# Turning the expert table's blocks elsewhere: 16 in the output projection, 8 in retrieval, and the sum of squares moved to GpSimd

## The chip, the cores and the metric

The kernel runs on one core of one Trainium2 chip. The metric is the device time of one execution in microseconds (us), the median over several runs. It is one program: a hand-written order of instructions for each engine (TensorE, VectorE, ScalarE, GpSimd, and SyncE, which issues most of the DMAs), tied together by semaphores.

## The reference, cut to what matters

The kernel computes one layer of a streaming encoder for 512 prompt and 32 sample frames (T = 544 columns), model width 2048. After attention and the recurrent branch, the part in question is

```python
h = x + mixed @ w_out                               # output projection
xn = rms_norm(h, norm2_g)                           # needs the sum of h*h over the 2048 channels
q = (xn @ w_q).reshape(n, 8, 2, 128)                # retrieval: 8 heads
s1, s2 = q[:, :, 0] @ k1.T, q[:, :, 1] @ k2.T
... top 16 of each, top 16 of their sums -> idx, gate
h = h + peer_ffn(...)                               # rows of peer_u and peer_v picked by idx
```

`peer_u` (16384 x 2048 floats) is used twice: block by block as a weight of dense products, and, for 160 of the frames, by gathering single rows. For the gathers it is needed in another layout than that of the blocks.

## The kernel before, in words

The activations stand transposed, 16 slices of 128 channels x 544 frames. A **unit** is one 128 x 2048 block of a weight (1 MB) times all of them: 16 slices, each in three products (high part by high, high by low, low by high) and, for 544 columns, in two pieces, so 96 matmuls. Each unit passes through `Stream` (L119): `load` (L145) brings the raw block into one of two buffers; `split_hi` (L150) on ScalarE rounds it to its high part `whi`; `split_lo` (L154) on GpSimd subtracts and gives `wlo`; then TensorE may start (L236). The load of unit c waits until unit c-2 is split, `split_hi` of unit c until TensorE has used unit c-2.

**Rows** (L178) is the other stream: 128 blocks of `peer_u` are loaded (L204), turned by VectorE in 32x32 squares (L210, `STREAM_TRANSPOSE`) and written to a buffer in DRAM, `u_d`, by four DMAs of 256 KB (L220), from where the experts gather rows. The 128 turns are spread over the stages: 64 in attention, 32 in the recurrent branch, 8 in `mix`, 24 in `out_projection`. All DMAs of both streams stand in SyncE's queue in the order in which the code writes them; a wait there holds back all behind it.

`out_projection` (L1436) has 16 units, in pairs. Unit 0's product is done at the end of `mix`, so its PE part begins with unit 1. For each unit n: VectorE adds the product to X (L1520) and then turns one block (even units) or two (odd units), over three buffers; ScalarE squares the slice (L1505) and splits the weight of unit n+2; TensorE adds the square of the slice before into a PSUM bank by a product with ones (L1477, `add_squares`), 18 times in all. SyncE begins with the four loads of X (L1451), three block loads and the weight of unit 2; then for each unit: the weight of unit n+2, and for each turn its four stores and the next block load. The weight of unit 2 is thus the eighth transfer, and that of unit 3 stands behind the stores of the first turn.

After it comes `norm` "n2", and then `retrieval` (L1525): for each of 8 heads, two units of `w_q` with 544 columns, ten small products with the keys, two dense units of `peer_u` with 384 columns (48 matmuls each); VectorE runs a long chain that finds the top 16 (L1707 to L1752); eight more dense units follow while VectorE makes the gates. After the eighth head ScalarE's exponential (L1681) stands behind six of these units.

Of the kernel before, what the change touches and what calls it, by code (L numbers as in the profile page):

```python
# [48 lines left out]

LEVELS = [2, 4, 8, 16, 32]  # L50

AT_ROWS, RW_ROWS, MX_ROWS, WO_ROWS = 64, 32, 8, 24
GBUF = 4


# [189 lines left out]
def build(nc, A, O):  # L245
    ctx = ExitStack()
    with ctx:
# [35 lines left out]
        with ExitStack() as back:  # L283
            sbk = lambda n, s, d=F32: back.enter_context(nc.sbuf_tensor(n, s, d))

            at_hh = nc.sbuf_base
            hh, hl = sbk("hh", [P, KB, T], F32R), sbk("hl", [P, KB, T], F32R)
            assert nc.sbuf_base == at_hh + 2 * KB * T * 4
            load_h = lambda a, b: h_d[a:b].rearrange("k p t -> p k t")
            rows = mix(nc, S, A, W.phase(base["mix"]), [A["w_out"][0], A["w_out"][1]], acc, psS, psR, hh, hl, gates_d, o_d, u_d, rows,  # L290
                       lambda pe: unit_product(pe, W.phase(base["out"]), 0, acc[0], hh, hl))
            with ExitStack() as ctx2:
                X = ctx2.enter_context(nc.sbuf_tensor("X2", [P, KB, T], F32))
                out_projection(nc, S, A, W.phase(base["out"]), [A["u"][0], A["u"][1]], acc, psS, hh, hl, X, u_d, rows)
                W2 = W.phase(base["n2"])

                def two_units(pe):
                    for c in range(2):
                        yield from dense_product(pe, W2, c, acc[c][:, 0, 0:TD], hh, hl)
                norm(nc, S, "n2", A, par, eps, psS, X, C_N2, hi=hh, lo=hl, keep=load_h, summed=True, W=W2, then=two_units,  # L300
                     following=[A["w_q"][0], A["w_q"][1]])
            IDX, GT = sbk("IDX", [P, P], U32), sbk("GT", [P, P])
            IDXB, GTB = sbk("IDXB", [P, DEC], U32), sbk("GTB", [P, DEC])
            with ExitStack() as picks:
                IT = picks.enter_context(nc.sbuf_tensor("IT", [P, 3, TD], F32))
                iota = picks.enter_context(nc.sbuf_tensor("iota", [P, P], F32))
                retrieval(nc, S, A, W.phase(base["retrieval"]), [A["u"][TAIL], A["u"][TAIL + 1]], acc, psS, psR, hh, hl, IT, iota, IDX, GT, IDXB, GTB, pre_d)
                gate_matrix(nc, S, A, W.phase(base["gates"]), [A["u"][PRE - 2], A["u"][PRE - 1]], acc, psS, psR, hh, hl, IT, iota, g_d, pre_d)
            H = sbk("H", [P, KB, T])
            experts(nc, S, A, W.phase(base["experts"]), accs, psS, psR, H, load_h, hh, hl, IDX, GT, IDXB, GTB, g_d, pre_d, u_d, at_hh)  # L310
            norm(nc, S, "nf", A, par, eps, psS, H, C_NF, out=O["yT"], summed=True)
# [1124 lines left out]
def out_projection(nc, S, A, W, ahead, acc, psS, mh, ml, X, u_d, before):  # L1436

    with ExitStack() as ctx:
        sb = lambda n, s, d=F32: ctx.enter_context(nc.sbuf_tensor(n, s, d))
        SQ, ones = sb("wo_SQ", [P, 2, T]), sb("wo_ones", [P, P])  # L1440
        UI, UO = sb("wo_UI", [P, 3, D]), sb("wo_UO", [P, 3, D])
        N = 2
        R = Rows(S, A, u_d, lambda b: UI[:, b, :], lambda b: UO[:, b, :], before, 1, 3, KB // N, 3, 3)
        halves = lambda t: t.rearrange("p (h t) -> p h t", h=2)
        flat = lambda k: X[:, bass.ds(k, 1), :].rearrange("p a t -> p (a t)")
        block = ctx.enter_context(nc.Block())

        @block.sync
        def _(sp):
            for q in range(4):  # L1450
                sp.dma_start(X[:, 4 * q:4 * q + 4, :], A["xT"][:, 4 * q:4 * q + 4, :]).then_inc(S[f"n1loaded{q}"], 16)  # L1451

            def block_pair(i, last):
                for u in range(N):
                    W.load(sp, ahead[u] if last else row(A["w_out"], N * i + u + 2), u + 2, N, i)
                    for c in range(1 + u):
                        R.store(sp, u + c, i)
                        if not last:
                            R.load(sp, u + c + 3, i)
            for c in range(3):  # L1460
                R.load(sp, c)
            with sp.Fori(0, KB // N - 1) as i:
                block_pair(i, False)
            block_pair(KB // N - 1, True)
            R.finish(sp)

        @block.gpsimd
        def _(pool):
            with pool.Fori(0, KB // N) as i:
                for u in range(N):  # L1470
                    W.split_lo(pool, u + 2, N, i)

        @block.tensor
        def _(pe):
            def add_squares(u, start=False):
                for half in range(2):
                    mm = pe.matmul(psS[:, half, 0:H2], ones[:, :], SQ[:, u, half * H2:(half + 1) * H2], start=start, stop=True,  # L1477
                                   skip_group_check=True)
                mm.then_inc(S["wo_summed"], 1)
            pe.wait_ge(S["wo_set"], 2)  # L1480
            add_squares(1, True)

            def block_pair(i, first=False):
                for u in range(N):
                    if not first or u:
                        pe.wait_ge(S["wo_sum"], N * i + u + 1)
                        for mm in unit_product(pe, W, u, acc[u], mh, ml, N, i):
                            pass
                        mm.then_inc(W.used, 2)
                    pe.wait_ge(S["wo_square"], N * i + u + 1)  # L1490
                    add_squares(1 - u)
            block_pair(0, True)
            with pe.Fori(1, KB // N) as i:
                block_pair(i)
            pe.wait_ge(S["wo_square"], KB + 1)
            add_squares(1)

        @block.scalar
        def _(act):
            act.sem_inc(S["wo_square"], 1)  # L1500
            with act.Fori(0, KB // N) as i:
                for u in range(N):
                    act.wait_ge(S["wo_sum"], N * i + u + 3)
                    act.wait_ge(S["wo_summed"], N * i + u + 1)
                    act.activation(SQ[:, u, :], flat(N * i + u), ACT.Square).then_inc(S["wo_square"], 1)  # L1505
                    W.split_hi(act, u + 2, N, i)

        @block.vector
        def _(dve):
            dve.memset(ones[:, :], 1.0).then_inc(S["wo_set"], 1)  # L1510
            dve.memset(SQ[:, 1, :], 0.0).then_inc(S["wo_set"], 1)
            dve.sem_inc(S["wo_sum"], 2)
            R.start(dve)
            for q in range(4):
                dve.wait_ge(S[f"n1loaded{q}"], 32)
                with dve.Fori(2 * q, 2 * q + 2) as i:
                    for u in range(N):
                        W.wait_used(dve, u, N, i)
                        h = halves(flat(N * i + u))
                        dve.tensor_tensor(h, acc[u][:, :, 0:H2], h, ALU.add).then_inc(S["wo_sum"], 1)  # L1520
                        for c in range(1 + u):
                            R.turn(dve, u + c, i)


def retrieval(nc, S, A, W, ahead, acc, psS, psR, hh, hl, IT, iota, IDX, GT, IDXB, GTB, pre_d):  # L1525

# [1 line left out]
    with ExitStack() as ctx:  # L1530
# [10 lines left out]
        SUM = sb("SUM", [P, 5, PH])  # L1541
        GEL = sb("tk_GEL", [P, 2, TD])
        IB = sb("tk_IB", [DEC, P], U32)
        N = 4
        OFF = [0, P, 2 * P, TD + DEC, TD]
        U0 = N * PH
# [8 lines left out]
        def _(sp):  # L1555
# [8 lines left out]
            def head(i, last):  # L1564
                for u in range(2):
                    W.load(sp, row(A["u"], 2 * i + (u + 2)), u + 2, N, i)
                for u in range(2):
                    W.load(sp, row(A["u"], 2 * PH + 2 + u) if last else row(A["w_q"], 2 * i + u + 2), u + 4, N, i)
                    sp.wait_ge(S["tk_q"], N * i + u + 5)
                    sp.dma_start(row(pre_d, 2 * i + (u + 2)), GEL[:, u, :]).then_inc(S[f"tk_kept{u}"], 16)  # L1570
            with sp.Fori(0, PH - 1) as i:
                head(i, False)
            head(PH - 1, True)
# [15 lines left out]
            for u in range(2):  # L1589
                sp.wait_ge(S[f"tk_kept{u}"], 16 * (TAIL // 2))  # L1590
            sp.wait_ge(S["few_moved"], 128)

        @block.gpsimd
        def _(pool):
# [95 lines left out]
        def _(dve):  # L1690
# [4 lines left out]
            dve.memset(POS[:, 4], 0).then_inc(S["tk_set"], 1)  # L1695
            dve.memset(TOP[:, 4], 0.0).then_inc(S["tk_set"], 1)
            dve.sem_inc(S["tk_head"], 1)
            dve.wait_ge(S["tk_set"], 5)
            dve.wait_ge(S["tk_cst"], 48)

            with dve.Fori(0, PH) as i:
                dve.wait_ge(S["tk_scores"], 2 * i + 4)
                ch = Chain(dve, S["tk_chain"], 13, i)

# [740 lines left out]
```

## Time and profile before

| what | us |
|---|---|
| median of 3 runs (4746.27 to 4752.65) | 4752.01 |
| the profiled execution, own time | 4754.84 |
| its span, first to last instruction | 4753.0 |
| TensorE busy in it | 4438.3 (93%) |
| `out_projection`, from its first DMA to the first of "n2" | 1840.61 to 2083.66 |
| `retrieval`, from its first DMA on | 2121.33 to about 2549 |

Times in the rows below are from the start of the profiled execution's span, in order as the engines ran. The clock of TensorE is given as a share of full speed, 1.00 for 2.4 GHz and 0.50 for 1.2 GHz.

### The profile page before, as it was taken

To read this page: it belongs to the slowest core of one execution; us is meant where nothing else is said; L and a number is where in the kernel's file an instruction comes from. 1 tells how busy PE (TensorE), PEld (TensorE's weight loads), DVE (VectorE), ACT (ScalarE), POOL (GpSimd) and SP (SyncE) were. 2 spreads that over 40 slices of the span, in tenths; PEclk is the share of its full clock that TensorE was granted. 3 is DMA by queue.
4 is the path that set the end of the run, shared out by engine and by line. 5 is a ranking of instruction groups with operands and counts; after the bars stand their busy time and mean duration, and the time that the engine had idled before them with its cause. 6 is when DMAs were issued, how large, how long until landed. Compare 5 with 4: busy or idle time off the path is not lost. (4 is left out here: it accounts for less than half of the span.)

```text
span 4753.0 us, 86860 instructions
## 1 busy us (share of the span) xinstructions
PE 4438.3 (93%) x33921; PEld 4299.0 (90%) x33921; DVE 3020.2 (64%) x4301; ACT 1365.6 (29%) x1786; POOL 2449.7 (52%) x929
## 2 busy tenths in 40 slices
PE   6999999999999898979999989999999999999997
PEld 5999888888888798969999989999999999999996
DVE  4333255555555432238996957777888888777786
ACT  3333322222222211122223333332322322333322
POOL 1332222222222133324443346779999999889885
PEclk8999999999999999989999999999999999999998
DMA  6999833444344376862233568888898998888884
GB/s 233 363 377 363 289 128 120 137 137 136 128 134 136 108 232 245 288 224 99 103 116 140 210 237 283 301 280 317 328 342 324 331 342 319 324 320 320 327 306 155
DMA packets 357708, 1141.23 MB, mean 240 GB/s; under 512 B 35088, under 2 KB 128656, under 8 KB 270224
## 3 DMA queue, kind: packets, MB, share of 16 engines
q1 hardware_dynamic: 294400, 780.38, 47.2%
q0 software_dynamic: 46080, 335.56, 18.7%
q10 hardware_dynamic: 17040, 22.58, 1.3%
q8 instruction: 142, 2.33, 0.2%
q14 instruction: 46, 0.38, 0.0%
HBM read 942.00 MB, written 195.32 MB: 239 GB/s over the span
## 5 line engine op out<-in xcount | busy, mean ns | idle before, releaser
L154 POOL TENSOR_TENSOR wlo<-raw,whi 128x2048 fp32r<-128x2048 f32 x174 | 804.0, 4621 | 1979.2 <-ACT whi L150 1680.2
L168 POOL TENSOR_TENSOR wlo<-raw,whi 128x1024 fp32r<-128x1024 f32 x424 | 1070.5, 2530 | 220.7 <-ACT whi L164 214.5
L164 ACT ACTIVATE whi<-raw 128x1024 fp32r<-128x1024 f32 x424 | 449.1, 1060 | 955.5 <-PE psR L236 402.7
L236 PE MATMUL accs<-xh,whi 128*128 128x272 f32 x2624 | 581.1, 303 | 56.5 <-POOL wlo L154 26.3
L236 PE MATMUL psS<-hh,whi 128*128 128x384 f32 x1600 | 545.6, 341 | 24.2 <-DVE clo L2272 19.5
L2307 DVE SCALAR_TENSOR_TENSOR H<-R,HD,H 128x2048 f32<-128x2048 f32 x127 | 563.6, 4438 | 2.1 <-DVE H L2307 0.5
L236 PE MATMUL accs<-xh,wlo 128*128 128x272 f32 x2624 | 547.7, 290 | 0.0
L236 PE MATMUL accs<-xl,whi 128*128 128x272 f32 x2624 | 546.8, 290 | 0.0
L236 PE MATMUL accs<-hh,whi 128*128 128x272 f32 (+1 forms) x1696 | 458.5, 320 | 48.6 <-POOL wlo L154 24.2
L236 PEld LDWEIGHTS accs<-xh,whi 128*128 128x128 f32 x2624 | 416.5, 190 | 86.9 <-issue 40.0
L236 PE MATMUL psS<-hl,whi 128*128 128x384 f32 x1344 | 455.4, 339 | 0.0
L236 PE MATMUL psS<-hh,wlo 128*128 128x384 f32 x1344 | 454.0, 338 | 0.0
L236 PE MATMUL accs<-hl,whi 128*128 128x272 f32 (+1 forms) x1696 | 443.2, 311 | 0.0
L236 PE MATMUL accs<-hh,wlo 128*128 128x272 f32 (+1 forms) x1696 | 442.8, 311 | 0.0
L236 PEld LDWEIGHTS accs<-xl,whi 128*128 128x128 f32 x2624 | 417.0, 191 | 0.0
L236 PEld LDWEIGHTS accs<-xh,wlo 128*128 128x128 f32 x2624 | 415.7, 191 | 0.0
L236 PE MATMUL psR<-chi,whi 128*128 128x384 f32 x1024 | 353.3, 345 | 62.1 <-POOL wlo L168 28.1
L150 ACT ACTIVATE whi<-raw 128x2048 fp32r<-128x2048 f32 x174 | 332.3, 1910 | 137.3 <-DMA raw<-in_w_out 71.7
L236 PE MATMUL psR<-chi,wlo 128*128 128x384 f32 x1024 | 349.2, 341 | 0.0
L236 PEld LDWEIGHTS accs<-hh,whi 128*128 128x128 f32 x1696 | 293.1, 191 | 59.1 <-POOL wlo L154 25.9
L236 PE MATMUL psS<-chi,whi 128*128 128x384 f32 x1024 | 344.9, 337 | 0.0
L236 PE MATMUL psS<-chi,wlo 128*128 128x384 f32 x1024 | 344.7, 337 | 0.0
(424 smaller groups left out, 8972.4 us busy)
## 6 DMA issues: line engine op xcount, KB each, us to landing
raw<-in_u SPq DMA_DIRECT2D x128, 1024.0 KB, 5.7
raw<-in_v SPq DMA_DIRECT2D x128, 1024.0 KB, 5.2
raw<-in_w_in SPq DMA_DIRECT2D x82, 1024.0 KB, 8.2
at_UI<-in_u SPq DMA_DIRECT2D x64, 1024.0 KB, 9.2
u_d<-at_UO SPq DMA_DIRECT2D x256, 256.0 KB, 6.5
wo_UI<-in_u SPq DMA_DIRECT2D x24, 1024.0 KB, 8.9
u_d<-wo_UO SPq DMA_DIRECT2D x96, 256.0 KB, 4.8
g_d<-STG SPq DMA_DIRECT2D x8, 3072.0 KB, 9.7
```

Source lines behind the costliest of these rows:

```text
L150: act.activation(self.hi[:, c % 2, :], self.raw[:, c % 2, :], ACT.Copy).then_inc(self.hi_done, 2)
L154: pool.tensor_tensor(self.lo[:, c % 2, :], self.raw[:, c % 2, :], self.hi[:, c % 2, :].bitcast(F32), ALU.subtract).then_inc(self.split_don ...
L164: act.activation(self.half(self.hi, c, h), self.half(self.raw, c, h), ACT.Copy).then_inc(self.hi_done, 1)
L168: pool.tensor_tensor(self.half(self.lo, c, h), self.half(self.raw, c, h), self.half(self.hi, c, h).bitcast(F32), ALU.subtract).then_inc(se ...
L236: mm = pe.matmul(out, w(k), x(k, n), start=a, stop=z)
L2307: dve.scalar_tensor_tensor(y, wide, coef, y, ALU.mult, ALU.add).then_inc(S["gx_done"], 1)
```

## The change

In `out_projection` every unit turns one block, so 16 in place of 24, over two buffers in place of three; 8 blocks are turned in `retrieval`, one a head, at the head's start on VectorE, with the stores and the next load at the end of the head's list on SyncE. SyncE's first transfers in `out_projection` are put in another order. The squares are added up by GpSimd into a tile `total` after each `split_lo`, and TensorE sums over the channels once, at the end: `total`, and the last square.

```diff
-AT_ROWS, RW_ROWS, MX_ROWS, WO_ROWS = 64, 32, 8, 24
+AT_ROWS, RW_ROWS, MX_ROWS, WO_ROWS, RT_ROWS = 64, 32, 8, 16, 8
...
-        UI, UO = sb("wo_UI", [P, 3, D]), sb("wo_UO", [P, 3, D])
+        UI, UO = sb("wo_UI", [P, 2, D]), sb("wo_UO", [P, 2, D])
...
-            for q in range(4):
+            def load_x(q):
                 sp.dma_start(X[:, 4 * q:4 * q + 4, :], ...)
-            def block_pair(i, last):
+            def block_pair(i, last, first=False):
                 for u in range(N):
-                    W.load(sp, ahead[u] if last else row(A["w_out"], N * i + u + 2), u + 2, N, i)
-                    for c in range(1 + u):
-                        R.store(sp, u + c, i)
-                        if not last:
-                            R.load(sp, u + c + 3, i)
-            for c in range(3):
-                R.load(sp, c)
-            with sp.Fori(0, KB // N - 1) as i:
+                    if not first:
+                        W.load(sp, ahead[u] if last else row(A["w_out"], N * i + u + 2), u + 2, N, i)
+                    R.store(sp, u, i)
+                    if not last:
+                        R.load(sp, u + 2, i)
+            load_x(0)
+            for u in range(N):
+                W.load(sp, A["w_out"][u + 2], u + 2)
+                R.load(sp, u)
+            for q in range(1, 4):
+                load_x(q)
+            block_pair(0, False, True)
+            with sp.Fori(1, KB // N - 1) as i:
                 block_pair(i, False)
...
         def _(pool):
+            pool.wait_ge(S["wo_set"], 3)
             with pool.Fori(0, KB // N) as i:
                 for u in range(N):
                     W.split_lo(pool, u + 2, N, i)
+                    pool.wait_ge(S["wo_square"], N * i + u + 1)
+                    pool.wait_ge(S["wo_summed"], N * i + u + 1)
+                    pool.tensor_tensor(total[:, :], total[:, :], SQ[:, 1 - u, :], ALU.add).then_inc(S["wo_summed"], 1)
...
-                    pe.wait_ge(S["wo_square"], N * i + u + 1)
-                    add_squares(1 - u)
...
+            pe.wait_ge(S["wo_set"], 3)
+            pe.wait_ge(S["wo_summed"], KB + 1)
+            add_squares(total, True)
             pe.wait_ge(S["wo_square"], KB + 1)
-            add_squares(1)
+            add_squares(SQ[:, 1, :], False)
...
+            dve.memset(total[:, :], 0.0).then_inc(S["wo_set"], 1)
...
-                        for c in range(1 + u):
-                            R.turn(dve, u + c, i)
+                        R.turn(dve, u, i)
... retrieval:
+        R = Rows(S, A, u_d, lambda b: UI[:, b, :], lambda b: UO[:, b, :], before, 1, TURNS, PH, TURNS, TURNS)
+                for c in range(TURNS):          # SyncE, end of a head
+                    R.store(sp, c, i)
+                    if not last:
+                        R.load(sp, c + TURNS, i)
+            for c in range(TURNS):              # SyncE, before the heads
+                R.load(sp, c)
+                for c in range(TURNS):          # VectorE, start of a head
+                    R.turn(dve, c, i)
```

TURNS is 1.

## Rows read from the trace of the kernel before

**Rows 1.** Waits from 1828 to 2084: engine line, waited for, us, times, longest.

```profile
PE accs L236 <- POOL wlo L154: 24.2, 4, 15.0
```

**Rows 2.** TensorE's timeline: start, us, instruction, idle before and its releaser.

```profile
1871.56 0.82 PE L236 MATMUL accs<-hh,whi 128*128 128x272 f32 x2 [15.00 <-POOL wlo L154]
...
1943.82 1.08 PE L1477 MATMUL psS<-wo_SQ,wo_ones 128*128 128x272 f32 x4
```

**Rows 3.** Busy time, TensorE clock, DMA share and GB/s of three stretches.

```profile
1871.00:1890.00 19.00, 18.44 (x125) 18.28 (x126) 2.94 (x2) 4.38 (x3) 5.16 (x3) 0.85 0.78 310
1844.00:1848.00 4.00, 4.00 (x34) 4.00 (x34) 0.72 (x1) 0.66 (x1) 0.00 (x0) 1.00 1.01 427
2211.00:2255.00 44.00, 44.00 (x312) 43.36 (x311) 40.36 (x154) 10.80 (x13) 18.61 (x4) 1.00 0.30 104
```

**Rows 4.** VectorE's timeline in the output projection, columns as before.

```profile
1846.03 0.72 DVE L1520 TENSOR_TENSOR X<-accs,X 128x544 f32 x1 [4.57 <-DMA X<-in_xT]
...
1886.40 0.72 DVE L1520 TENSOR_TENSOR X<-accs,X 128x544 f32 x1 [21.62 <-PE accs L236]
...
1899.34 0.72 DVE L1520 TENSOR_TENSOR X<-accs,X 128x544 f32 x1 [9.99 <-PE accs L236]
...
1925.86 4.50 DVE L210 STREAM_TRANSPOSE wo_UO<-wo_UI 128x2048 f32<-128x2048 f32 x2
...
2070.05 0.72 DVE L1520 TENSOR_TENSOR X<-accs,X 128x544 f32 x1 [9.99 <-PE accs L236]
```

**Rows 5.** The DMAs that SyncE issued there, same columns.

```profile
1844.52 0.34 SPq L145 DMA_DIRECT2D raw<-in_w_out  x1
...
1864.94 0.86 SPq L145 DMA_DIRECT2D raw<-in_w_out  x1
...
1889.52 2.91 SPq L220 DMA_DIRECT2D u_d<-wo_UO  x4
...
1893.94 0.89 SPq L145 DMA_DIRECT2D raw<-in_w_out  x1
...
2073.01 7.31 SPq L220 DMA_DIRECT2D u_d<-wo_UO  x8
2083.66 3.52 SPq L337 DMA_DIRECT2D h_d<-X  x4
```

**Rows 6.** ScalarE's timeline there.

```profile
1864.96 1.91 ACT L150 ACTIVATE whi<-raw 128x2048 fp32r<-128x2048 f32 x1 [17.34 <-DMA raw<-in_w_out]
...
1874.11 1.91 ACT L150 ACTIVATE whi<-raw 128x2048 fp32r<-128x2048 f32 x1 [6.70 <-DMA raw<-in_w_out]
...
1903.15 1.92 ACT L150 ACTIVATE whi<-raw 128x2048 fp32r<-128x2048 f32 x1 [2.23 <-DMA raw<-in_w_out]
```

**Rows 7.** ScalarE in retrieval, timeline.

```profile
2223.16 0.62 ACT L1655 ACTIVATE tk_QT<-accs 128x544 f32<-128x544 f32 x1 [9.72 <-PE accs L236]
...
2235.19 0.62 ACT L1655 ACTIVATE tk_QT<-accs 128x544 f32<-128x544 f32 x1 [9.60 <-PE accs L236]
```

**Rows 8.** VectorE in retrieval, timeline.

```profile
2195.27 0.87 DVE L1707 MAX8 V<-SC 128x8 f32<-128x128 f32 x4 [2.22 <-ACT SC L1667]
...
2528.60 0.82 DVE L1765 TENSOR_REDUCE SUM<-OUT 128x40 f32<-128x640 f32 x1 [21.60 <-ACT OUT L1681]
```

**Rows 9.** Transfers from 1840 to 2084: SyncE's queue: packets, MB, share of 16 engines.

```profile
q1 hardware_dynamic: 20160, 71.57, 85.9%
```

**Rows 10.** GpSimd's timeline there.

```profile
1905.21 4.59 POOL L154 TENSOR_TENSOR wlo<-raw,whi 128x2048 fp32r<-128x2048 f32 x1 [10.68 <-ACT whi L150]
1924.50 4.54 POOL L154 TENSOR_TENSOR wlo<-raw,whi 128x2048 fp32r<-128x2048 f32 x1 [14.69 <-ACT whi L150]
...
2073.57 4.50 POOL L154 TENSOR_TENSOR wlo<-raw,whi 128x2048 fp32r<-128x2048 f32 x1 [4.91 <-ACT whi L150]
```

**Rows 11.** GpSimd's smaller split on the page's list of groups: busy, mean ns.

```profile
L168 POOL TENSOR_TENSOR wlo<-raw,whi 128x1024 fp32r<-128x1024 f32 x424 | 1070.5, 2530 | 220.7 <-ACT whi L164 214.5
```

**Rows 12.** SyncE in retrieval, timeline.

```profile
2212.71 6.00 SPq L145 DMA_DIRECT2D raw<-in_u  x2
```

More of the change, by code:

```diff
@@ L293, in build @@
                 X = ctx2.enter_context(nc.sbuf_tensor("X2", [P, KB, T], F32))
-                out_projection(nc, S, A, W.phase(base["out"]), [A["u"][0], A["u"][1]], acc, psS, hh, hl, X, u_d, rows)
+                rows = out_projection(nc, S, A, W.phase(base["out"]), [A["u"][0], A["u"][1]], acc, psS, hh, hl, X, u_d, rows)
                 W2 = W.phase(base["n2"])
@@ L306, in build @@
                 iota = picks.enter_context(nc.sbuf_tensor("iota", [P, P], F32))
-                retrieval(nc, S, A, W.phase(base["retrieval"]), [A["u"][TAIL], A["u"][TAIL + 1]], acc, psS, psR, hh, hl, IT, iota, IDX, GT, IDXB, GTB, pre_d)
+                retrieval(nc, S, A, W.phase(base["retrieval"]), [A["u"][TAIL], A["u"][TAIL + 1]], acc, psS, psR, hh, hl, IT, iota, IDX, GT, IDXB, GTB, pre_d, u_d, rows)
                 gate_matrix(nc, S, A, W.phase(base["gates"]), [A["u"][PRE - 2], A["u"][PRE - 1]], acc, psS, psR, hh, hl, IT, iota, g_d, pre_d)
@@ L1439, in out_projection @@
         sb = lambda n, s, d=F32: ctx.enter_context(nc.sbuf_tensor(n, s, d))
-        SQ, ones = sb("wo_SQ", [P, 2, T]), sb("wo_ones", [P, P])
-        UI, UO = sb("wo_UI", [P, 3, D]), sb("wo_UO", [P, 3, D])
+        SQ, ones, total = sb("wo_SQ", [P, 2, T]), sb("wo_ones", [P, P]), sb("wo_total", [P, T])
+        UI, UO = sb("wo_UI", [P, 2, D]), sb("wo_UO", [P, 2, D])
         N = 2
-        R = Rows(S, A, u_d, lambda b: UI[:, b, :], lambda b: UO[:, b, :], before, 1, 3, KB // N, 3, 3)
+        R = Rows(S, A, u_d, lambda b: UI[:, b, :], lambda b: UO[:, b, :], before, 1, N, KB // N, 2, 2)
         halves = lambda t: t.rearrange("p (h t) -> p h t", h=2)
@@ L1471, in _, with add_squares @@
                     W.split_lo(pool, u + 2, N, i)
+                    pool.wait_ge(S["wo_square"], N * i + u + 1)
+                    pool.wait_ge(S["wo_summed"], N * i + u + 1)
+                    pool.tensor_tensor(total[:, :], total[:, :], SQ[:, 1 - u, :], ALU.add).then_inc(S["wo_summed"], 1)
         @block.tensor
         def _(pe):
-            def add_squares(u, start=False):
+            def add_squares(x, start):
                 for half in range(2):
[L1477 to L1481, printed above, removed]
+                    pe.matmul(psS[:, half, 0:H2], ones[:, :], x[:, half * H2:(half + 1) * H2], start=start, stop=not start)
             def block_pair(i, first=False):
@@ L1511, in _ @@
             dve.memset(SQ[:, 1, :], 0.0).then_inc(S["wo_set"], 1)
+            dve.memset(total[:, :], 0.0).then_inc(S["wo_set"], 1)
+            dve.sem_inc(S["wo_summed"], 1)
             dve.sem_inc(S["wo_sum"], 2)
@@ L1520, in _, with retrieval @@
                         dve.tensor_tensor(h, acc[u][:, :, 0:H2], h, ALU.add).then_inc(S["wo_sum"], 1)
-                        for c in range(1 + u):
-                            R.turn(dve, u + c, i)
-def retrieval(nc, S, A, W, ahead, acc, psS, psR, hh, hl, IT, iota, IDX, GT, IDXB, GTB, pre_d):
+                        R.turn(dve, u, i)
+    return R.after
+def retrieval(nc, S, A, W, ahead, acc, psS, psR, hh, hl, IT, iota, IDX, GT, IDXB, GTB, pre_d, u_d, before):
     with ExitStack() as ctx:
@@ L1543, in retrieval @@
         IB = sb("tk_IB", [DEC, P], U32)
+        TURNS = RT_ROWS // PH
+        UI, UO = sb("tk_UI", [P, TURNS, D]), sb("tk_UO", [P, TURNS, D])
+        R = Rows(S, A, u_d, lambda b: UI[:, b, :], lambda b: UO[:, b, :], before, 1, TURNS, PH, TURNS, TURNS)
         N = 4
@@ L1591, in _ @@
             sp.wait_ge(S["few_moved"], 128)
+            R.finish(sp)
         @block.gpsimd
@@ L1697, in _ @@
             dve.sem_inc(S["tk_head"], 1)
+            R.start(dve)
             dve.wait_ge(S["tk_set"], 5)
```

## The prediction

> **What bounds the kernel now.** The page's busy shares come first: TensorE is busy 93% of the span, so what counts is where it stands still, where its clock is low, and what it does that it needn't. The list of waits for the output projection gives the first: TensorE waited 24.2 us in 4 times for a split weight, 15.0 of them at once [rows 1]. The timeline of TensorE has that stop in front of unit 2, which starts at 1871.56 [rows 2]; the clock of the stretch behind it is 0.85 of full, so part of it ran at 1.2 GHz [rows 3]. VectorE's additions mark the ends of the units. Units 2 and 3 lie 12.94 us apart. From unit 2 (1886.40) to unit 15 (2070.05) there are 183.65 us for 13 units, 14.13 each [rows 4]: 13 x 12.94 is 168.2, so 15.4 us more went into the three other stops and their slow restarts. Unit 2 itself took 14.84 from its start to its addition, where a unit at full clock takes 12.03 and 0.3 to the addition: the slow restart cost 2.5.
>
> What the stop waits for is read backwards. GpSimd's split needs ScalarE's, which needs the load. The weight of unit 2 was issued at 1844.52 and landed at 1864.96; the one issued at 1864.94 landed at 1874.11; that issued at 1893.94 at 1903.15 [rows 5, 6]. The first stood behind four loads of X and three blocks. So SyncE's order and the DMA engines' time bound this stage beside TensorE. In retrieval TensorE is busy 44.00 of 44 us at clock 1.00 [rows 3], two units 12.03 apart [rows 7], and VectorE idles 2.22 a head [rows 8].
>
> **What a transfer costs.** With loads alone 427 GB/s were moved at a full share of the engines [rows 3]: 1.05 MB takes 2.5 us, a quarter of X (1.11 MB) 2.6. SyncE's queue moved 71.57 MB in 244 us at a share of 85.9%, 209.6 us of engine time [rows 9]. 46.4 MB of it are loads (108.7 us) and 2.6 us belong to the first store of "n2"; 98.3 us stay for 24 blocks stored, 4.1 each. Are they served in order of issue? Between the landings at 1864.96 and 1874.11, 9.15 us, lay one block stored, one loaded and one weight: 4.1 + 2.5 + 2.5 = 9.1. And X's first quarter landed at 1846.03 though nearly all of eight transfers stood behind it [rows 4]. So I take them as served in order.
>
> **The change, part by part**, on the clock of the trace before.
>
> *Start.* Unit 1 now waits for VectorE's three memsets, about 1842.0 (an estimate), and two sums of squares fall away in front of it. It ends at 1854.1. X's first quarter is in at 1846.0, the weight of unit 2 one load later, 1848.5. Then 1.9 us on ScalarE, 0.15 between, 4.6 on GpSimd [rows 6, 10]: unit 2 starts at 1855.2, not 1871.56. It ends at 1867.2, unit 3 (weight in at about 1853.5) at 1879.3.
>
> *Unit 4* is late next. Its weight now stands behind the rest of X and two turns' stores and loads. The first 8.65 MB are through at 1864.4, as before; then 4.1 + 2.5 + 4.1 + 2.5 + 2.5 = 15.7 us: landed 1880.1, split 1886.8. TensorE waits 7.5 us and pays 2.3 for the slow restart: unit 4 ends at 1901.1.
>
> *Steady state.* The squares leave TensorE: four matmuls a unit [rows 2], 12.94 - 12.03 = 0.91 us [rows 4, 7]. Each unit now has the list that even units had: store after the turn, load, weight. With unit n's product ending some 0.33 before its addition (1886.07), the weight of unit n+3 was issued at +7.87, landed at +17.1 and, by 1.92 + 0.14 + 4.59, was split at +23.7 [rows 4, 5, 6, 10]. Two units after it TensorE wants it, at 2 x 12.03 = 24.06. That is 0.3 us of slack, on DMA engines busy 4.1 + 2.5 + 2.5 = 9.1 of 12.03 us. I take 12.03 a unit and 1 us in all for hiccups, with 0 to 3 as bounds. Units 5 and 6 have weights in by 1898, ahead of need. So unit 15 ends at 1901.1 + 11 x 12.03 + 1 = 2034.4, its addition at 2034.8: **35.3 us** earlier than 2070.05.
>
> *GpSimd's addition.* The trace has none of 544 columns. Its splits take 2.53 us for 1024 columns [rows 11] and 4.6 for 2048 [rows 10], 2.05 per 1024 and 0.45 fixed: 1.55 us; bounds 0.5 (VectorE needs 0.72 for one of that size [rows 4]) and 2.53. GpSimd is free 7.4 us a unit, so it is hidden; without that cover it would be 1.55 x 15. Behind its waits stands the next split, and ScalarE's square waits for the addition one unit back, while its own weight lands later still.
> The two engines' work does not collide here: the GpSimd split at 1924.50 took its 4.54 us beside two turns from 1925.86, 2.25 each, as undisturbed ones [rows 4, 10]. The Trainium skill ("SBUF — State Buffer", "SBUF: two separate sides") says that the port which both share is an exclusive lock, taken by a VectorE instruction in a two-port mode or with two SBUF inputs. By that rule turns, one input each, would not block it; if they did, at 2.3 a unit, the slack above would be gone and the sum would lose up to 11 x 1 us. The trace agrees with the rule for turns.
>
> *End.* Before, the stage ended 13.6 us after unit 15's addition: two turns, eight stores issued until 2080.3, landing at 2083.6 [rows 5]. Now four stores: about +10. The chain of squares is longer: the last split ends at 2078.07, 8.0 after the addition [rows 10], then 1.55 on GpSimd, about 2.6 for eight matmuls at a lower clock (four spanned 1.08 at full [rows 2]), 0.3 to leave: +12.5. **1 us** gained, bounds 0 to 2.
>
> *Retrieval*, 8 turns of 2.3 us. VectorE has 2.22 idle a head, so it slips at most some 0.2 a head, 1.6 in all. At the end it waits 21.6 us for ScalarE's exponential [rows 8], which stands behind TensorE's units: hidden, and it would be 1.6 on the path without. On SyncE four stores and a load go ahead of the next head's weights, 4.4 us of issuing as from 1889.52 to 1893.94 [rows 5]: issued at 2217 in place of 2212.71 [rows 12], landed 9.2 later at 2226.2, split at 2232.9. TensorE wants that weight at 2238, after two units and the key products (unit ends at 2223 and 2235 [rows 7]). Slack 5 us, so nothing. Behind the last head the wanted time is nearer, since dense units (384 columns, two thirds of the work) follow each other: 0 to 2 us. Cost **0.5**.
>
> Sum: 35.3 + 1 - 0.5 = 35.8 us of the execution profiled, 4754.84, thus 4719.0. That one stands 2.8 above the median of the runs shown; from 4752.0 the same step gives **4716**.
>
> **Rivals.** *The slack of 0.3 us does not hold* and the loop stays bound by transfers: each unit has a turn now, and the stores of one begin while the weight before still lands. Then the pace stays near the present mean less the squares, 14.13 - 0.91 = 13.22: 11 x 1.19 = 13 us less gain, and up to 10 more for slow restarts, 4729 to 4739. For it: four stops in the present stage. Against: the even units' own list landed at +17.1. 15%.
>
> *Transfers issued together share the engines.* Then the early weights land with the rest near 1864 and unit 2 stops as before; unit 4 does not. 16.4 lost and 9.8 of unit 4's won back: 4723. Only X's early landing speaks against it. 7%.
>
> *Retrieval's weights come late* (the other sign): in each head the weight behind the new stores lands 7.5 us later than reckoned, eats the 5 us of slack, stops TensorE 2.5 and costs 2.3 for the restart, 4.8 x 8 = 38 us: 4754. It decides from 5 us on. The DMA engines are at 0.30 there [rows 3], so 4%.
>
> *The squares were hidden anyway.* Units at 12.94 and not 12.03, 13 x 0.9 = 12 less: 4728. Against it, TensorE had no idle time around them. 3%.
>
> **How the numbers follow.** The forecast's own case holds 71%, 4710 to 4722 by its bounds (hiccups 2, end 1, retrieval 1.5, unit 4 by 3, and 3 for the runs' own scatter). The range reaches into the first rival: 4708 to 4734. The kernel's runs lie 6.4 us apart (0.13%), so 0.2% or 9.5 us is what a measurement tells: over that faster in all cases but the third and the worst of the first, 0.94; within 0.02; slower 0.04.
>
> **What would show it.** Unit 2's product starting near 1855 and not 1871; one stop near 1879 of 6 to 8 us, at a lower clock behind it; additions of L1520 12.03 apart; no matmuls of ones until the end; a GpSimd addition of 1.5 us; "n2" starting some 36 us earlier and the distance from there to the end unchanged within 2 us; VectorE's wait for scores in retrieval near zero. Additions 13 or more apart, or ScalarE's wait for weights in every unit, would show the first rival; a TensorE stop in each head the third.

## The result and the profile after

The changed kernel took 4714.05 us (median of 6 runs, 4701.9 to 4724.4) beside 4751.37 for the kernel before (6 runs, 4739.6 to 4755.9): ratio 0.9915, 95% interval 0.990 to 0.993. The forecast was 4716. The profiled execution took 4719.02, of which its span is 4717.1; the same step worked out against the profiled execution of before had given 4719.0.

Three stretches make up the difference: the output projection (first transfer of X to the first of "n2"), from there to the last scores that ScalarE copies in retrieval, and the rest.

| stretch, us | before | after | difference | forecast |
|---|---|---|---|---|
| ahead of the projection | 1840.61 | 1840.41 | -0.2 | 0 |
| output projection | 243.05 | 206.57 | -36.5 | -36.3 |
| "n2" and retrieval | 460.73 | 465.53 | +4.8 | +0.5 |
| from there to the end | 2208.61 | 2204.59 | -4.0 | 0 |

The total agrees so closely because two misses cancel: retrieval lost more than forecast, and the last stretch, which the change doesn't touch, came out 4 us shorter. It scatters: in the thirteen profiles taken after the one of before it lasted from 2196.9 to 2211.2 us, and the stretch ahead of the projection from 1830.7 to 1850.2. So below it is stretches that are compared, and the medians only beside them.

VectorE's additions mark the ends of the units (start, us, instruction, idle before it and its releaser):

```profile
1845.88 0.72 DVE L1528 TENSOR_TENSOR X<-accs,X 128x544 f32 x1 [4.04 <-DMA X<-in_xT]
...
1867.36 0.72 DVE L1528 TENSOR_TENSOR X<-accs,X 128x544 f32 x1 [8.37 <-PE accs L236]
...
1879.38 0.72 DVE L1528 TENSOR_TENSOR X<-accs,X 128x544 f32 x1 [5.54 <-PE accs L236]
...
1900.86 0.72 DVE L1528 TENSOR_TENSOR X<-accs,X 128x544 f32 x1 [18.54 <-PE accs L236]
...
1912.89 0.73 DVE L1528 TENSOR_TENSOR X<-accs,X 128x544 f32 x1 [9.09 <-PE accs L236]
...
2033.15 0.72 DVE L1528 TENSOR_TENSOR X<-accs,X 128x544 f32 x1 [9.08 <-PE accs L236]
```

Unit 2 now ends at 1867.36 where before it ended at 1886.40 [rows 4]. Between unit 3 and unit 4 lie 21.48 us, the one long stop that is left; from unit 4 to unit 15 there are 132.3 us for 11 units, 12.03 each. TensorE's own timeline has the two waits in the product that are left, in front of unit 2 and unit 4, where the kernel before had four, 24.2 us in all [rows 1, 2]:

```profile
1854.88 0.52 PE L236 MATMUL accs<-hh,whi 128*128 128x272 f32 x2 [1.89 <-POOL wlo L154]
...
1885.80 0.82 PE L236 MATMUL accs<-hh,whi 128*128 128x272 f32 x2 [6.58 <-POOL wlo L154]
...
2042.76 2.15 PE L1486 MATMUL psS<-wo_total,wo_ones 128*128 128x272 f32 x4 [9.78 <-POOL wo_total L1480]
2044.71 2.02 PE L1486 MATMUL psS<-wo_SQ,wo_ones 128*128 128x272 f32 x4
```

Where the stop comes from is seen on SyncE and ScalarE. Weights are L145, stores L220:

```profile
1859.02 3.28 SPq L220 DMA_DIRECT2D u_d<-wo_UO  x4
1862.34 2.05 SPq L204 DMA_DIRECT2D wo_UI<-in_u  x1
1864.76 0.44 SPq L145 DMA_DIRECT2D raw<-in_w_out  x1
...
1908.36 0.86 SPq L145 DMA_DIRECT2D raw<-in_w_out  x1
```

```profile
1879.19 1.91 ACT L150 ACTIVATE whi<-raw 128x2048 fp32r<-128x2048 f32 x1 [10.25 <-DMA raw<-in_w_out]
...
1917.57 1.92 ACT L150 ACTIVATE whi<-raw 128x2048 fp32r<-128x2048 f32 x1 [3.10 <-DMA raw<-in_w_out]
```

The weight of unit 4 could be loaded as soon as unit 2 was split, at 1854.8; it was issued at 1864.76, behind eight stores and two block loads, and landed at 1879.19. A later weight, issued at 1908.36, landed 9.2 us after.

In retrieval it is the last head where time is lost. SyncE, ScalarE, GpSimd and TensorE there, in this order:

```profile
2438.34 2.97 SPq L220 DMA_DIRECT2D u_d<-tk_UO  x4
2441.68 3.35 SPq L145 DMA_DIRECT2D raw<-in_u  x2
...
2449.20 1.92 ACT L150 ACTIVATE whi<-raw 128x2048 fp32r<-128x2048 f32 x1 [2.77 <-DMA raw<-in_u]
...
2451.26 10.20 POOL L154 TENSOR_TENSOR wlo<-raw,whi 128x2048 fp32r<-128x2048 f32 x2 [6.77 <-ACT whi L150]
...
2456.79 0.45 PE L236 MATMUL accs<-hh,whi 128*128 128x384 f32 x1 [2.54 <-POOL wlo L154]
```

The weight for the third of the eight dense units behind the heads stands behind the last head's four stores. (The expectation of run 7 calls that unit the second; its result is copied out at 2467.15, behind those of 2445.94 and 2454.28.) The weight lands 2.77 us after ScalarE is free for it; TensorE then stops 2.54 us and runs on at a granted clock of 0.86. Dense units there follow each other 8.34 to 8.51 us apart; this one came 12.87 after the one before it, so this place costs 4.4 of the 4.8 us.

### The profile page after: what moved, and what is told of

Its sections match the earlier page's. It is cut to its first block and busy times, and to the rows that moved or that the text cites. A ratio compares the mean times of both kernels' runs of the same rounds, so it can differ in the third digit from the quotient of the medians.

```text
span 4717.1 us, 86755 instructions
## 1 busy us (share of the span) xinstructions
PE 4421.7 (94%) x33857; PEld 4283.7 (91%) x33857; DVE 3016.3 (64%) x4302; ACT 1366.8 (29%) x1786; POOL 2476.0 (52%) x945
## 5 line engine op out<-in xcount | busy, mean ns | idle before, releaser
L210 DVE STREAM_TRANSPOSE at_UO<-at_UI 128x2048 f32<-128x2048 f32 x64 | 147.9, 2311 | 303.6 <-DMA at_UI<-in_u 303.6
```

The costliest lines, as they stand in the source:

```text
L210: dve.transpose(self.uo(b).rearrange("p (e k j) -> p e k j", e=4, j=32), self.ui(a).rearrange("p (k e j) -> p e k j", e=4, j=32)).then_inc ...
```

## The experiments

"Stage" below is the output projection in the sense of the table. "After" is the changed kernel, from which all but the ninth start.

**1. The squares back on TensorE**, 16 turns kept.

```diff
-                    pool.tensor_tensor(total[:, :], total[:, :], SQ[:, 1 - u, :], ALU.add).then_inc(S["wo_summed"], 1)
...
+                    pe.wait_ge(S["wo_square"], N * i + u + 1)
+                    add_squares(1 - u)
```

> The changed kernel with the squares summed on TensorE again, unit by unit, and no addition on GpSimd. Theory (squares stood on TensorE's path): additions of L1520's kind 12.94 us apart and not 12.03, the output projection from its first DMA to the first of n2 10 to 11 us longer than the 206.6 us of the changed kernel (13 more on the units, 2 to 3 less at the end, where the chain over GpSimd goes), 4724 us. Rival (hidden squares): units 12.03 apart, 206 to 208 us, 4714.

Measured: 4730.17 us (6 runs), ratio 0.9944 (0.9925 to 0.9963); stage 212.12, 5.5 longer than after's. Units are 12.94 apart in place of 12.03, so the four matmuls do stand on the path. But the end, from unit 15's addition to "n2", took 9.57 against 13.83: 4.3 shorter, more than the 2 to 3 expected. The squares on GpSimd give 9.8 us over the units and take 4.3 back at the end. The stage came out only 5.5 longer where 10 to 11 were expected: besides the end, unit 4's stop was 3.26 us in this run and 6.58 in after. Slower units leave its weight more time, which fits this; no run tests it alone.

**2. The old order of the first transfers**: X, the blocks, then the weights.

```diff
-            load_x(0)
-            for u in range(N):
-                W.load(sp, A["w_out"][u + 2], u + 2)
-                R.load(sp, u)
-            for q in range(1, 4):
-                load_x(q)
+            for q in range(4):
+                load_x(q)
+            for u in range(N):
+                R.load(sp, u)
```

> The changed kernel with the first order of transfers of before: X's four loads, the block loads, then the weights. Theory (transfers are served in order, and the stop at unit 4 is the price of the weights brought forward): unit 2 starts near 1869 after a stop of 13 to 15 us, the stop before unit 4 (6.6 us and its slow restart) is gone, the stage 6 to 8 us longer than 206.6, 4721. Rival (the stop at unit 4 has another cause and stays): 14 to 16 us longer, 4729.

Measured: 4728.06 us (10 runs), ratio 0.9943 (0.9926 to 0.9961); stage 213.94, 7.4 longer, as expected. One stop of 15.85 us in front of unit 2, and none at unit 4: the new order moves part of a stop from unit 2 to unit 4, and is worth what it takes away on the whole. The total fits the rival's 4729 better than the theory's 4721, but this profile had the stage as the theory said, and the stop that the rival keeps was not there.

**3. 24 turns in the projection, none in retrieval**, the rest as after.

```diff
-                    R.store(sp, u, i)
-                    if not last:
-                        R.load(sp, u + 2, i)
+                    for c in range(1 + u):
+                        R.store(sp, u + c, i)
+                        if not last:
+                            R.load(sp, u + c + 3, i)
```

> The changed kernel with 24 turns in the output projection, one and two a unit over three buffers, and none in retrieval. Theory: two units then ask 2 x 2.5 + 3 x 2.5 + 3 x 4.1 = 24.8 us of the DMA engines in 24.06 us, and stops come back: additions 13.2 us apart in the mean, the stage near 220 us; retrieval's last stop (2.5 us and its slow restart, 4.5 in all) is gone; 4723 in all. Rival (the first order and the squares gave the gain, the number of turns nothing): the stage 206 to 208 us, 4710.

Measured: 4740.86 us (10 runs), ratio 0.9967 (0.9953 to 0.9981); stage 232.93, 26.4 longer than after's and far above both expectations. TensorE waited four times, 26.7 us; three additions lie 28.54, 19.46 and 18.98 us behind the one before, all others from unit 3 on 12.03, and the end took 18.81. In retrieval the dense unit behind the last head is 8.51 from the one before it again. With this order on SyncE the third turn of a pair costs a great deal; whether the DMA engines or the place in the queue makes it cost that was the question of the next run.

**4. 24 turns, and each weight issued one unit earlier.** The weight of unit n+3 goes ahead of the stores of unit n.

```diff
-                        W.load(sp, ahead[u] if last else row(A["w_out"], N * i + u + 2), u + 2, N, i)
-                    R.store(sp, u, i)
+                        W.load(sp, ahead[0] if ending and u else row(A["w_out"], N * i + u + 3), u + 3, N, i)
+                    for c in range(1 + u):
+                        R.store(sp, u + c, i)
```

> As the kernel with 24 turns here, and each weight's load issued one unit earlier on SyncE, ahead of that unit's stores. Theory (a weight is late because of its place in the queue, and beyond that the DMA engines' time counts): the mean pace is the DMA engines' 24.8 us for two units, 12.4 each, no stop at unit 4, the stage 200 to 205 us; 4708 in all. Rival (24 turns need their stops whatever the order): near 220 us, 4723.

Measured: 4707.21 us (4 runs), ratio 0.9905 (0.9875 to 0.9934); stage 203.05. Behind the short wait in front of unit 2 (1.8 us here) one stop of 4.4 us at unit 4 is left, and all units behind it are 12.02 or 12.03 apart. So the stage lies in the expected range by two misses: a stop that the theory hadn't, and a pace of 12.03 where it had 12.4. The windows of two pairs (length, busy time of TensorE, its weight loads, VectorE, ScalarE, GpSimd, then granted clock, DMA share, GB/s):

```profile
1928.10:1952.20 24.10, 24.10 (x194) 24.10 (x194) 8.08 (x5) 4.94 (x4) 11.83 (x4) 1.00 0.97 345
1952.20:1976.20 24.00, 24.00 (x194) 24.00 (x193) 8.08 (x5) 4.94 (x4) 11.83 (x4) 1.00 0.95 337
```

The share is 0.95 to 0.97 with three stores and five loads in two units. Loads at 2.5 leave 24.06 x 0.96 - 12.5 = 10.6 us for three stores, 3.5 each, not 4.1. So the engines are not the bound of the projection even with 24 turns; the place of the weights in SyncE's queue is.

**5. After, run once more on another chip**, for the runs 6 to 8.

> The changed kernel itself, beside the three variants of this chip. 4714 us, the output projection 206.6 us from its first DMA to the first of n2.

Measured: 4724.27 us (6 runs, 4712.2 to 4732.1), ratio 0.9944 (0.9929 to 0.9960); stage 206.57 again to the hundredth, the dense unit behind the last head 11.35 from the one before. The stretches ahead of the projection and behind retrieval were together 10 us longer than in the first profile, so the ratio of one and the same kernel was 0.9915 in one set of runs and 0.9944 in the other.

**6. 16 turns, each weight one unit earlier.**

```diff
-                    if not first:
-                        W.load(sp, ahead[u] if last else row(A["w_out"], N * i + u + 2), u + 2, N, i)
+                    if last and not u:
+                        W.load(sp, ahead[1], u + 3, N, i)
+                    elif not last and not (first and not u):
+                        W.load(sp, ahead[0] if ending and u else row(A["w_out"], N * i + u + 3), u + 3, N, i)
                     R.store(sp, u, i)
```

> The changed kernel with each weight's load in the output projection issued one unit earlier on SyncE, ahead of that unit's stores and block load. Theory (the stop at unit 4 is the weight's place behind two turns' transfers): no stop before unit 4, additions 12.03 apart from unit 2 on, the stage 198 us in place of 206.6, 4705. Rival (the DMA engines' backlog of the start sets unit 4, whatever the order): the stop stays within 2 us of its 6.6, 4713.

Measured: 4711.28 us (5 runs), ratio 0.9924 (0.9910 to 0.9937); stage 198.03, as expected; no stop at unit 4. (The same edit in run 8 left one of 1.42 us there.) With the weights ahead, 24 turns (run 4) cost 5.0 us more than 16, not 26.4: unit 4 is 6.2 us later after unit 3 there, and unit 2 came 1.7 later here.

**7. The last head's stores behind all weights.**

```diff
-                for c in range(TURNS):
-                    R.store(sp, c, i)
-                    if not last:
-                        R.load(sp, c + TURNS, i)
+                if not last:
+                    for c in range(TURNS):
+                        R.store(sp, c, i)
+                        R.load(sp, c + TURNS, i)
...
             blocks(AFTER // 2 - 1, True)
+            R.store(sp, 0, PH - 1)
```

> The changed kernel with the stores of retrieval's last turn put behind all of retrieval's weight loads. Theory (they hold back the weight of the second dense unit after the heads): the stop of 2.5 us there and its slow restart are gone, the eight dense units' evacuations 8.4 us apart throughout, 4.5 us less behind n2's start. Rival (the split on GpSimd is late by VectorE's two-input instructions, not by the weight): the stop stays, or half of it.

Measured: 4717.44 us (6 runs), ratio 0.9935 (0.9921 to 0.9948); from "n2" to the last scores 460.45 where the two profiles of after have 465.53 and 463.60, and the dense units are 8.34 to 8.51 apart all through. So the late weight is the cost. A turn a head on VectorE costs nothing that shows: the five profiles without turns in retrieval (before and runs 3, 4, 9 and 11) have 459.63 to 462.88 in this stretch. GpSimd's splits at this place:

```profile
2445.00 4.67 POOL L154 TENSOR_TENSOR wlo<-raw,whi 128x2048 fp32r<-128x2048 f32 x1 [3.90 <-ACT whi L150]
2453.35 4.84 POOL L154 TENSOR_TENSOR wlo<-raw,whi 128x2048 fp32r<-128x2048 f32 x1 [3.67 <-ACT whi L150]
```

They take 4.7 and 4.8 us here and 10.20 for two in after.

**8. The edits of 6 and 7 together.**

> Both edits together. Theory: the gains add, the stage 198 us and 4.5 us less behind it, 4700 to 4702. Rival (time won before the experts is given back there): 4708 or more, with the stages as in theory.

Measured: 4704.16 us (5 runs), ratio 0.9905 (0.9891 to 0.9918); stage 198.48, "n2" to the last scores 462.81. The latter is 2 us above run 7's with no dense unit late; that is within what profiles without any turns differ in this stretch. The stage kept a stop of 1.42 us at unit 4, with the weights one unit ahead, and the total lies between the theory's 4700 to 4702 and the rival's 4708.

**9. The order alone, on the kernel before**: 24 turns, squares on TensorE, nothing in retrieval; X's first quarter and the first weights first, and each weight one unit earlier.

```diff
-            for q in range(4):
-                sp.dma_start(X[:, 4 * q:4 * q + 4, :], ...)
-            for c in range(3):
-                R.load(sp, c)
+            load_x(0)
+            for u in range(N):
+                W.load(sp, A["w_out"][u + 2], u + 2)
+                R.load(sp, u)
+            R.load(sp, 2)
+            for q in range(1, 4):
+                load_x(q)
...
-                    W.load(sp, ahead[u] if last else row(A["w_out"], N * i + u + 2), u + 2, N, i)
+                        W.load(sp, ahead[0] if ending and u else row(A["w_out"], N * i + u + 3), u + 3, N, i)
                     for c in range(1 + u):
                         R.store(sp, u + c, i)
```

> The kernel before (24 turns in the output projection, squares on TensorE, nothing turned in retrieval) with SyncE's list alone changed: the changed kernel's first order of transfers, and each weight's load one unit earlier. Theory (the stops were the weight's place in the list): units 12.94 apart throughout but for a stop of at most 5 us before unit 4, the stage 210 to 213 us in place of 243, 30 us less than before in all, 4720. Rival (fewer turns or the squares are needed to end the stops): the three stops of 4.5 to 6 us remain, the stage 225 us or more, 4734.

Measured: 4722.17 us (6 runs), ratio 0.9941 (0.9925 to 0.9958); stage 211.72, 31.3 shorter than before's. In place of stops of 24.2 us there are these:

```profile
PE accs L236 <- POOL wlo L154: 1.1, 2, 0.8
```

**10. GpSimd's addition ahead of its split**, the rest as after.

```diff
-                    W.split_lo(pool, u + 2, N, i)
                     pool.wait_ge(S["wo_square"], N * i + u + 1)
                     pool.wait_ge(S["wo_summed"], N * i + u + 1)
                     pool.tensor_tensor(total[:, :], total[:, :], SQ[:, 1 - u, :], ALU.add).then_inc(S["wo_summed"], 1)
+                    W.split_lo(pool, u + 2, N, i)
```

> The changed kernel with GpSimd's addition put ahead of the split of the same round. Theory (the stage's end is held by the chain last split, addition, sums on TensorE): the end comes 9.6 us after the last addition to X, with the stores, and not 13.8; the stage 202.5 us, 4 less in all. Rival (the stores or the leaving of the stage hold it as much): 206 us.

Measured: 4713.67 us (6 runs), ratio 0.9924 (0.9908 to 0.9940); stage 202.09, and the end 9.54. (The total doesn't show the 4 us: the two sets of after had 0.9915 and 0.9944.) `total` is ready 0.5 us after unit 15's addition to X begins; TensorE waits 0.80 us for it and runs the products with ones, where in after TensorE stood idle for 9.78 us first and took 2.15 for the first four of them, at a granted clock of 0.50:

```profile
2033.12 1.16 PE L1486 MATMUL psS<-wo_total,wo_ones 128*128 128x272 f32 x4 [0.80 <-POOL wo_total L1479]
2034.12 1.18 PE L1486 MATMUL psS<-wo_SQ,wo_ones 128*128 128x272 f32 x4
```

**11. 24 turns with all edits of the order**: weights ahead, addition first, and the last two quarters of X behind the first pair's transfers.

```diff
-            for q in range(1, 4):
-                load_x(q)
+            load_x(1)
             block_pair(0, False, True)
+            for q in range(2, 4):
+                load_x(q)
```

> 24 turns in the output projection, none in retrieval; each weight one unit earlier, the two last quarters of X loaded behind the first pair's transfers, GpSimd's addition ahead of its split. Theory: no stop at all, units 12.03 apart on DMA engines that are nearly full, the stage 193 to 197 us (two turns at its end), retrieval undisturbed, 4698. Rival (at a DMA share of 0.95 to 1.03 any shift brings stops back): the stop at unit 4 moves to a later unit, 200 us or more, 4706.

Measured: 4711.96 us (6 runs), ratio 0.9925 (0.9909 to 0.9941); stage 203.90, not the 193 to 197 of the theory: the rival's case. Unit 4 is on time, unit 5 is 5.5 us late in its place (17.5 from unit 4): its weight was issued at 1873.62, behind eight stores, two block loads and the two quarters of X that follow the weight of unit 4. The last of them:

```profile
1865.79 3.61 SPq L220 DMA_DIRECT2D u_d<-wo_UO  x4
1869.44 1.19 SPq L204 DMA_DIRECT2D wo_UI<-in_u  x1
1870.67 2.58 SPq L1451 DMA_DIRECT2D X<-in_xT  x2
1873.62 0.52 SPq L145 DMA_DIRECT2D raw<-in_w_out  x1
```

The end took 13.59, as before's 13.61, and not 9.54 as in run 10: two turns and their eight stores stand behind unit 15 and not one turn and four. That is the second price of 24 turns.

**12. 16 and 8 turns with all edits of the order**, and the last head's stores late: the edits of 6, 7, 10 and 11 on after.

> 16 turns here and 8 in retrieval, with every edit of order: weights one unit earlier, the two last quarters of X later, the addition ahead of the split, retrieval's last stores late. Theory: the stage 193 to 194 us, no stop, 4697. Rival (as the kernel with 24 turns, but 8 turns in retrieval cost 2 us or more by TensorE's stops there): 4700 or more.

Measured: 4705.59 us (6 runs), ratio 0.9908 (0.9892 to 0.9923); stage 192.72 as expected, 50.3 shorter than before's, and "n2" to the last scores 460.91. Its only waits for a split weight from unit 2 on are these:

```profile
PE accs L236 <- POOL wlo L154: 1.8, 1, 1.8
```

By stretches it is the best version. By the total it is on a par with runs 4 and 8 (0.9905 each, with intervals that overlap), and 9 us above the 4697 expected: what it has gained in the projection over run 8, 5.8 us, the medians don't show.

## Why the prediction was right

**Unit 2** was forecast to start at 1855.2 and started at 1854.88. Run 2 shows the other side: with the old order it waits 15.85 us. That X's quarters and the weights are served in order was the assumption. The weight of unit 2 was there for ScalarE at 1848.21 (forecast 1848.5), with three quarters of X issued behind it by 1844.5. So the rival by which transfers issued together share the engines is ruled out:

```profile
1848.21 1.92 ACT L150 ACTIVATE whi<-raw 128x2048 fp32r<-128x2048 f32 x1 [0.74 <-DMA raw<-in_w_out]
```

**Unit 4**: weight landed at 1879.19 (forecast 1880.1), stop 6.58 (7.5). With what the slow restart took, unit 4 came 21.48 behind unit 3 in place of 12.03: 9.4 us, forecast 9.8. The stop isn't fixed: the same transfers in the same order gave 6.14 in run 5, 6.27 in run 10 and 4.37 in run 7. The granted clock of the stretch around it, and of one further on:

```profile
1880.00:1900.00 20.00, 14.20 (x92) 14.20 (x93) 2.33 (x2) 3.67 (x3) 11.69 (x4) 0.74 0.73 265
...
1949.00:1973.00 24.00, 24.00 (x194) 24.00 (x193) 5.88 (x4) 5.15 (x4) 11.38 (x5) 1.00 0.87 261
```

**The pace** was 12.03, and of the 1 us for hiccups nothing was needed: one unit came 12.45 after the last, the next 11.6. The squares gave the 0.91 a unit that the rows had promised (run 1). The slack of 0.3 us held, and it was as thin as forecast: the weight of unit 7, issued at 1908.36, was split by 1924.23, and unit 6, behind which TensorE needs it, ended some 0.33 us before its addition at 1924.91.

```profile
1919.63 4.60 POOL L154 TENSOR_TENSOR wlo<-raw,whi 128x2048 fp32r<-128x2048 f32 x1 [9.31 <-ACT whi L150]
```

So the rival by which this slack fails is ruled out for 16 turns. With 24 turns under the same order the stops did come back (run 3).

**One price in the working was wrong**, though the sum for the steady state didn't suffer. A store of 4.1 us of the DMA engines' time was worked out from their busy share over the stage. (2.6 us were taken off for a store of "n2", but the 71.57 MB are used up by the stage's own 46.4 MB of loads and 25.2 MB of stores; without that step it is 4.2.) Run 4 leaves 3.5, and by 4.1 it should have gone at 12.4 a unit; it went at 12.03. The changed kernel's window, two stores and four loads in 24 us at a share of 0.87 (1949 to 1973, above), gives 20.9 - 10.0 = 10.9 us by the same sum, 5.4 a store, where the forecast had the engines busy for 9.1 of 12.03 us, 0.76. One fixed price fits neither: the share is nearly as high with two stores as with three, so it can't be divided into prices, and how much room it leaves has to be tried.

What bound the kernel before was not the engines' time but the list on SyncE: each weight stood behind stores that themselves wait for a turn, and a turn for an addition. Run 9 puts a number on it: 31.3 us, beside the 36.5 that the change gained in this stage, are to be had by an order alone, with 24 turns and the squares where they were. That order is more than the change's own, as it also puts each weight one unit earlier; the change's own order with 24 turns (run 3, with the squares on GpSimd) gained 10.1. And fewer turns are worth 26.4 us under the change's own order (run 3) and 5.0 once the weights go ahead (runs 4 and 6). The parts don't add up, because each removes the same stops.

**GpSimd's addition**: 1.35 us, forecast 1.55, hidden in the loop. It cost at the end: the term there was forecast as a gain of 1 us, bounds 0 to 2, and was a loss of 0.2 (13.83 against 13.61). The first part of the chain was right: the last split ended 8.2 us and GpSimd's last addition 9.5 us after unit 15's addition to X. The eight products with ones were taken at 2.6 us and took 4.0, from 2042.76 to 2046.73, at a granted clock of 0.50: TensorE had stood for 9.78 us. Runs 1 and 10 show that 4.3 us lay in this chain: the four stores alone allow 9.55.

**Retrieval** is the term that was mis-sized most: 0.5 with bounds of 0 to 2, measured 4.8 in this profile and 2.9 in the second one. As profiles without turns scatter by 3 us in this stretch, the place itself is the better measure: 4.4 us in this profile, 2.8 in the second, 4.3 to 4.4 in runs 1, 2, 6 and 10. The eight heads are as forecast. VectorE's waits for scores were 2.22 us a head [rows 8], and now, from "n2" to the last head:

```profile
DVE SUM L1787 <- ACT OUT L1700: 28.0, 1, 28.0
DVE V L1729 <- ACT SC L1686: 25.3, 2, 21.7
```

The wait for scores comes up only twice, once ahead of the first head's chain (21.7) and once later (3.6), and no longer in every head; TensorE waited in none from 2121 to 2440; and VectorE's last wait is 28.0 where it was 21.6, of which the late dense unit makes 4.4. So the turns lie in idle time. The place was named ("behind the last head the wanted time is nearer"), the size was not. Of the 4.4 us between the two dense units 2.54 are TensorE's stop; the other 1.8 went into the restart, at a granted clock of 0.86:

```profile
2450.00:2462.00 12.00, 9.46 (x46) 9.14 (x45) 11.97 (x10) 3.40 (x3) 10.20 (x2) 0.86 0.41 150
```

Run 7 takes the cause away, the weight behind the stores, and both parts go. The rival with a stop in each head did not occur.

GpSimd's two splits took 10.20 us there, against 4.64 and 4.80 at the same place before: the first, which TensorE waited for, 5.48, so that 0.8 of the stop are its share. Beside them VectorE makes the gates. After, and then before:

```profile
2448.61 0.24 DVE L1759 CAST PHF<-PH 128x160 f32<-128x160 uint32 x1
2448.89 3.44 DVE L1764 TENSOR_TENSOR CA<-PHF,iota 128x256 f32<-128x256 f32 x10
2452.37 12.06 DVE L1770 TENSOR_TENSOR CA<-CA,IF 128x256 f32<-128x256 f32 x10
```

```profile
2484.82 4.53 DVE L1737 CAST PHF<-PH 128x160 f32<-128x160 uint32 x1
2489.38 3.44 DVE L1742 TENSOR_TENSOR CA<-PHF,iota 128x256 f32<-128x256 f32 x10
2492.86 7.86 DVE L1748 TENSOR_TENSOR CA<-CA,IF 128x256 f32<-128x256 f32 x10
```

Ten products that no split delays take 3.44 us. Taken one by one, the long groups hold single instructions that last about as long as a whole split. Before, beside the split of 2484.61 to 2489.25 the cast lasted 4.53 us in place of 0.24, and beside the next one, from 2492.96 to 2497.76, one product did:

```profile
2493.20 4.83 DVE L1748 TENSOR_TENSOR CA<-CA,IF 128x256 f32<-128x256 f32 x1
```

After, both splits fall beside the products, and two of these last 4.66 and 4.80. VectorE's three groups end 15.9 us (before) and 15.8 us (after) from their start: it lost the same to GpSimd, to other instructions. The Trainium skill ("SBUF — State Buffer", "SBUF: two separate sides") says that the port pair of the two goes to whichever starts first, for its whole instruction, and that the other then waits; on VectorE's side this holds for an instruction in a two-port mode or with two SBUF inputs. The trace agrees for the products, which have two inputs and lasted until the split's end. The cast has one input and lasted until its split's end too; that it runs in a two-port mode no view here shows. Nor does the number of inputs alone settle it for the turns of the projection, as the prediction had it; what shows that they don't collide are the splits that a turn of 2.3 us overlapped, at 1850.28 (4.56 us) and 1881.25 (4.50): neither they nor the turns were longer than others.

**The total** came out at the forecast because the last stretch was 4.0 us shorter in this profile, which nothing in the change explains. In the second set of runs (run 5) it was not, and the ratio was 0.9944 and not 0.9915. The direction and the size of the stage's gain are shown; the total's agreement to 2 us is partly luck.

## What to carry to other kernels

An issuing queue is a chain: put a load that the critical engine waits for ahead of everything in that queue that waits for something else, one unit earlier where its own buffer allows it, before making transfers fewer. The share of busy DMA time says little on this: 0.86 over the stage with 24 us of stops, 0.96 in a stretch of run 4 with none.
When work is moved to another stage, check that stage's last iteration as well as its steady one; a slack of 5 us a head was less than nothing behind the last head.
When a sum is moved to a slower engine because it is hidden in the loop, look at the loop's end: put it ahead of that engine's other work, or its last step stands bare.

## What the runs showed of the hardware

- **Mixed transfers.** Three stores of 1 MB and five loads fit in 24 us at a DMA share of 0.95 to 0.97, 337 to 345 GB/s, where loads alone ran at 427 [rows 3]. Two stores and four loads in 24 us stand at 0.87 and 261 GB/s. With loads at 2.5 us the first leaves 3.5 us a store, the second 5.4: the busy share is not a sum of fixed prices.
- **Restarts of TensorE differ after like stops, and the granted clock tells them apart.** In front of unit 2 TensorE stood for 1.8 to 2.1 us in ten profiles. In seven of them the unit came 13.2 to 13.5 us after the one before it, in runs 6, 7 and 11 14.9. The clock of unit 2 in after (1.89 us idle) and in run 7 (2.02 us):

```profile
1854.90:1867.00 12.10, 12.10 (x96) 12.10 (x97) 2.31 (x1) 2.46 (x2) 7.15 (x3) 1.00 1.03 378
1853.00:1866.90 13.90, 13.87 (x98) 13.87 (x99) 2.31 (x1) 2.46 (x2) 7.20 (x3) 0.88 1.02 384
```

  The length of the stop doesn't decide it: the clock fell behind 1.79 us in run 6 and held behind 2.12 in run 8. Nothing here tells beforehand which it will be.
- **VectorE beside GpSimd's splits.** A single VectorE instruction of 0.24 to 0.42 us lasted 4.5 to 4.8 us when it met a split, a cast with one input as well as products with two. The 32x32 turns did not: where a turn and a split overlapped, they took 2.3 and 4.5 to 4.6 us, as apart.
